# A step of a hybrid decoder with 64 experts: sample rows in slots of their own, gathered rows turned by VectorE, part of one expert's weights loaded earlier

## The reference

```python
scores = sigmoid(t @ w_router)                     # 64 experts
e_idx  = top 6 of (scores + b_router) in the best 4 of 8 groups
w      = scores[e_idx] / sum * 2.5
for each expert e: y += w[:, e] * (silu(t @ gate[e]) * (t @ up[e])) @ down[e]   # gate, up: 1024 x 256; down: 256 x 1024
y     += shared expert (same shape);  x = x + g2 * rms_norm(y)
```

## Time and profile before

| | |
|---|---|
| median of 3 runs | 930.7 us (930.54 to 934.95) |
| profiled execution | span 935.2 us |
| busy in it | PE 876.3, DVE 329.2, ACT 199.0, POOL 155.1 us |
| DMA | 325.47 MB, mean 348 GB/s |

### The profile page before, as it was taken

The page is one execution under the profiler, slowest core; times in us unless marked ns, Lnnn a source line. Parts: engine busy times, 40 slices in busy tenths (PEclk is TensorE's granted clock), DMA queues, the critical chain, the costliest instruction groups (busy, mean ns, idle before and its releaser), DMA issues.

```text
span 935.2 us, 18109 instructions
## 1 busy us (share of the span) xinstructions
PE 876.3 (94%) x7475; PEld 564.8 (60%) x7475; DVE 329.2 (35%) x795; ACT 199.0 (21%) x507; POOL 155.1 (17%) x185
## 2 busy tenths in 40 slices
PE   5899999997899899999899999999999999989987
PEld 3788888875666668756755555554555555444442
DVE  2315580047334598536322322222121221222214
ACT  2000110316222299024011111111111111101012
POOL 0000000022467000000312121121212212212110
PEclk9999999999899999999999999999999999999998
DMA  9966766737499947999999999999999999999993
GB/s 370 379 230 242 286 261 238 301 97 256 148 290 345 377 168 260 419 417 403 351 413 412 416 424 418 420 417 424 419 422 415 426 416 422 419 422 419 421 404 137
DMA packets 61237, 325.47 MB, mean 348 GB/s; under 512 B 16321, under 2 KB 25394, under 8 KB 40610
## 3 DMA queue, kind: packets, MB, share of 16 engines
q1 hardware_dynamic: 47218, 305.53, 81.4%
q0 software_dynamic: 12176, 18.56, 5.9%
q10 hardware_dynamic: 1760, 0.20, 0.2%
HBM read 326.65 MB, written 15.81 MB: 366 GB/s over the span
## 4 chain that ended last, share of the span: by engine, by line
PE 36%; DMA 13%; DVE 1%; SPq 0%; issue 0%; ACT 0%
PE bank L2428 19%; DMA slot_b<-in_w_e 13%; PE bank L2368 9%; PE bank L2379 4%; PE bank L2344 3%; PE bank L2438 1%; PE bank L2414 1%; SPq L1699 0%; DVE slot_b L2750 0%; DVE slot_b L2758 0%; PE bank L2398 0%; PE bank L2406 0%; ACT slot_b L2579 0%; DVE ht L2660 0%; DVE con L2652 0%
## 5 line engine op out<-in xcount | busy, mean ns | idle before, releaser
L420 PE MATMUL bank<-h,ring 128*128 128x264 f32 x608 | 138.4, 388 | 0.5 <-PE bank L420 0.3
L420 PEld LDWEIGHTS bank<-h,ring 128*128 128x128 f32 x608 | 114.6, 190 | 21.9 <-issue 2.6
L2652 DVE TENSOR_TENSOR con<-scales_of,bank 64x256 f32<-64x256 f32 x64 | 27.2, 425 | 270.5 <-ACT scales_of L2561 270.5
L1719 POOL DMA_INDIRECT xg<-tok_rows,tab_g x32 | 32.4, 1013 | 330.1 <-PE bank L2344 298.9
L2561 ACT ACTIVATE scales_of<-bank 64x256 f32<-64x256 f32 x64 | 24.2, 378 | 282.8 <-PE bank L2428 282.8
L2428 PE MATMUL bank<-done_out,xt 128*64 128x256 f32 x704 | 78.8, 381 | 3.7 <-DMA done_out<-in_w_e 2.8
L2428 PE MATMUL bank<-ring,xt 128*64 128x256 f32 x672 | 78.2, 386 | 0.0
L2428 PEld LDWEIGHTS bank<-done_out,xt 128*64 128x64 f32 x704 | 50.3, 137 | 33.9 <-issue 5.7
L2428 PEld LDWEIGHTS bank<-ring,xt 128*64 128x64 f32 x672 | 46.9, 138 | 35.7 <-issue 11.8
L2379 PE MATMUL bank<-sq,con 64*128 64x512 f32 x256 | 65.6, 609 | 0.0
L2368 PE MATMUL bank<-ring,ht 128*32 128x512 f32 x288 | 65.3, 595 | 0.0
(11 more groups left out here) (493 smaller groups left out, 1326.0 us busy)
## 6 DMA issues: line engine op xcount, KB each, us to landing
ring<-in_w_units SPq DMA_DIRECT2D x25, 2048.0 KB, 11.4
done_out<-in_w_e SPq DMA_DIRECT2D x22, 2048.0 KB
ring<-in_w_e SPq DMA_DIRECT2D x20, 2048.0 KB
slot_b<-in_w_e SPq DMA_DIRECT2D x11, 2048.0 KB
slot_f<-in_w_e SPq DMA_DIRECT2D x10, 2048.0 KB
ring<-in_w_e SPq DMA_DIRECT2D x16, 1024.0 KB
slot_b<-in_w_e SPq DMA_DIRECT2D x9, 1024.0 KB
done_out<-in_w_e SPq DMA_DIRECT2D x9, 1024.0 KB
```

Of the source, the lines that this page charges most:

```text
L420: mm = pe.matmul(bank[:, t % NB, 0:T], w[:, j, k, :], h[:, k, :], start=(k == 0), stop=(k == KD - 1))
L1719: pool.indirect_dma_start(xg[q % AHEAD][:, :], None, tok_rows, bass.IndirectOffsetOnAxis(ap=tab_g[:, q:q + 1].bitcast(U32), axis=0), bound ...
L2652: dve.tensor_tensor(hh[e % 2][:, :], sg[e % 2][:, :], bank[LB:2 * LB, 4 + e % 2, 0:FE], ALU.mult).then_inc(hh_ready, 1)
```

## The change

- The sample tokens no longer stand in the lists. Of every 32 places of an expert and half, 28 (`LS`) are for listed prompt tokens and 4 (`OWN`) hold always the same 4 sample rows, which are stored into xg once (8 small DMAs on POOL). VectorE adds their results to acc, with their weights of that expert, which may be zero (`add_own`). choice_rows, its scatters and its reading back are gone.
- The gathered rows are turned by VectorE in 32 x 32 blocks, straight from xg into one of two xt (`turn_rows`), PE's turn stays for the first pair only. ScalarE makes the copies `half_out` instead of VectorE.
- The two blocks of routing and expert loop are one, without the barrier between them.
- slot_f moves to a fixed place and holds only a gu. Of expert 5's, columns 1536 to 4096 of each partition (five eighths, 1.31 MB) are loaded in the state stage, the rest where the whole was. dn has 6 slots; expert 6's goes to w_sd.

```diff
-ROUNDS = -(-(P + TS) // HB)
+OWN = 4
+LS = HB - OWN
+ROUNDS = 1 + -(-(P - LS) // HB)
...
-SLOTS, DSLOTS = 6, 7
+SLOTS, DSLOTS = 6, 6
...
+AT_SLOT_F = AT_SAMP - 4 * GU
+EARLY_GU = 3 * 2 * FE
...
                         load_row(0)
                         load_row(1)
+                        sp.dma_start(slot_f[:, EARLY_GU:GU], io["w_e"][5][:, EARLY_GU:GU]
+                                     ).then_inc(small_in, 16)
                         sp.wait_ge(y_done6, 2)
...
-                        load_gu(sp, 5)
-                        load_dn(sp, 6)
+                        sp.dma_start(gu_at[5][:, 0:EARLY_GU], io["w_e"][5][:, 0:EARLY_GU]).then_inc(gu_in[5], 16)
...
+                        for i in range(AHEAD):
+                            for x4 in range(4):
+                                pool.dma_start(xg[i][x4 * HB + LS:(x4 + 1) * HB, :], rows_s[x4 % 2 * OWN:x4 % 2 * OWN + OWN, :]).then_inc(own_in, 16)
+                        pool.wait_ge(own_in, 16 * 4 * AHEAD)
...
+                        def turn_rows(q, h):
+                            if h == 0:
+                                dve.wait_ge(x_in[q % AHEAD], 16 * (q // AHEAD + 1))
                             if q >= 2:
+                                dve.wait_ge(gu_done, 2 * q - 3 + h)
                             for l in range(2):
+                                at = slice(h * LB + l * HB, h * LB + (l + 1) * HB)
+                                rows = xg[q % AHEAD][at, :].rearrange("p (k r c) -> p r k c", k=KD, r=4)
+                                for r in range(4):
+                                    ins = dve.transpose(xt[q % 2][32 * r:32 * r + 32, :, at], rows[:, r, :, :])
+                            ins.then_inc(xt_ready, 1)
...
+                        def add_own(q):
+                            dve.wait_ge(y_ready, 2 * q + 2)
+                            if q == 0:
+                                dve.wait_ge(own_ready, 1)
+                                ins = dve.tensor_scalar(acc[:, :], yo[q % NYO], own_w[:, q:q + 1], None, ALU.mult)
+                            else:
+                                dve.wait_ge(acc_ready, q)
+                                ins = dve.scalar_tensor_tensor(acc[:, :], yo[q % NYO], own_w[:, q:q + 1], acc[:, :], ALU.mult, ALU.add)
+                            ins.then_inc(acc_ready, 1)
```

More of the change, by code:

```diff
@@ L115 @@
                   ("valid", NT), ("later", NBLK - NE),
[L116 removed]
+                  ("count", MAXOVER), ("same_head", NH), ("code", NT), ("second", 1)):
     CONSTS[_name] = (_at, _at + _n)
@@ L1770, in _, with overflow @@
+                                        bounds_check=TP - 1, oob_is_err=False).then_inc(x_in[q % AHEAD], 16)
+            def overflow(eng):
+                eng.wait_ge(over_ready, 1)
+                return eng.value_load(over[0:1, 0:1], min_val=0, max_val=MAXOVER)
+            with nc.Block() as block:
                     @block.sync
@@ L1914, in _ @@
[L1914 to L1923 removed]
+                        pe.wait_ge(key_ready, 2)
@@ new lines, in combine @@
+                        def combine(n):
+                            q, h = n // 2, n % 2
+                            pe.wait_ge(y_ready, n + 1)
+                            pe.wait_ge(w_ready, q + 1)
+                            for l in range(2):
+                                at = slice(l * LB, (l + 1) * LB)
+                                mm = pe.matmul(bank[:, 2 * l + h, :], wmat[q % 2][at, :], yo[q % NYO][at, h * 512:(h + 1) * 512],
+                                               start=(q == 0), stop=(q == NPAIR - 1))
+                            mm.then_inc(comb_done, 1)
@@ new lines, in counts, with spread_weights @@
+                        def counts():
+                            for i, a in enumerate((0, 2)):
+                                mm = pe.matmul(bank[0:1, 7, (4 + i) * NE:(5 + i) * NE], ones[:, 0:1], chosen[:, a, :], start=True, stop=True)
+                            mm.then_inc(cnt_done, 1)
+                        def spread_weights():
+                            pe.wait_ge(comb_in, 32)
+                            pe.wait_ge(wgt_ready, 1)
+                            for i in range(2):
+                                mm = pe.matmul(bank[:, 7, 256:256 + NPAIR], own_at[i], wgt[0:TS, 1, i::2], start=(i == 0), stop=(i == 1))
+                            mm.then_inc(spread_done, 1)
@@ new lines, in _ @@
+                        act.wait_ge(fresh, 1)
+                        rows_half(0)
+                        rows_half(1)
+                        for e in range(NE):
+                            act.wait_ge(gu_done, e + 1)
+                            if e >= 2:
+                                act.wait_ge(hh_ready, e - 1)
+                            act.activation(sg[e % 2][:, :], bank[0:LB, 4 + e % 2, 0:FE], ACT.Silu).then_inc(sg_ready, 1)
+                            if e % 2 and e >= 2:
+                                half_out(e - 3)
+                                half_out(e - 2)
+                            if e == NE // 2:
+                                more = overflow(act)
@@ L1988, in _ @@
+                        act.wait_ge(sum_done, 1)
+                        square(4, slice(0, P), bank[:, 4, 0:QD], junk)
+                        act.wait_ge(sum_done, 2)
+                        act.activation(inv[:, 2:3], bank[:, 5, 0:1], ACT.Sqrt, bias=eps, scale=1.0 / D).then_inc(inv_rooted, 1)
+                        act.wait_ge(y_done, 3)
+                        for c in (2, 3):
+                            store(act, io["y"][TP:T, c * QD:(c + 1) * QD], y_s[32 * c:32 * c + TS, :])
                     @block.vector
```

1125 lines of the change are left out of this document (494 added, 631 removed).

## The result

The changed kernel takes **935.8 us** (median of 17 runs, 932.3 to 940.8), the kernel before 931.6 us (median of 17 beside it, 929.0 to 935.0). The ratio is **1.0044, 95% interval 1.0031 to 1.0058: 4.1 us slower**. The forecast was 927.8 us with 923.5 to 931.5 as its range, so it missed in direction as well as in range.

What follows compares the result with a forecast made beforehand. The queue of weights, at about 420 GB/s, was taken as the bound. The terms -3.1 - 1.2 + 1.9 + 0.3 - 1.4 + 0.65 = -2.9 us, from the 930.7 us median, gave 927.8 us, range 923.5 to 931.5.

Steps and rivals of the forecast that it cites:

- The bound: From 374 us the weight queue moves about 420 GB/s; remaining bytes, its idle time and the tail set the time.
- Step 1: Expert loop: PE no longer turns gathered rows, 1.36 us less a pair, counted for nothing except once in the tail.
- step 2: Expert loop: VectorE's turning takes 0.41 us each; costs nothing up to 0.67 us, a period of 14.4 us.
- cost 0: Expert loop: VectorE's 8.7 us latency fits PE's 7.06 + 3.57 us of work, 1.9 us left, so no cost.
- Step 3: State stage: 1.31 MB of expert 5's gate and up loaded early, fully hidden, -3.1 us.
- Step 4: Expert loop: scatters and gathering of the sample rows go away, 0.39 MB, -1.2 us (bounds 0.9 and 1.5).
- the own rows: Around 455 us: storing the sample rows once, 128 KB in 8 small stores of 16 KB, +0.3 us.
- Step 5: Around 455 us: less queued ahead, queue idles 5.5 us against 3.65, +1.9 us; later work joins without a gap.
- Hole 1: The weight queue's idle stretch before about 455 us, forecast between 444.8 and 455.3, 5.5 us idle against 3.65 before.
- the rival of small stores: Before the first gather: POOL's small stores hold it, gate_up(0) 3.5 us late, gain given back, 931.3 us; chance 0.14.
- Step 6: Tail: PE's path ends 3.1 us after the last weights, before 4.2, -1.4 us; later square-root table load, +0.65 us.
- The table load: Tail: ScalarE loads the square root's table behind the last copy, 1.28 us; squares start 1.1 us later, +0.65 us.

Runs made afterwards that it cites:

- experiment 11: Changed kernel plus 8 or 16 unused VectorE turnings of 32 x 192 in each pair from the fourth on: 937.3 us (one run) and 1080.7 us.
- experiment 1: Changed kernel with the first pair's gate products ahead of VectorE's turning of the second pair's rows: 1.0017 to the kernel before.
- experiment 8: Changed kernel plus 18 unused PE matmuls between the second gate and up and the turning of the products: 1.0015 to the kernel before.
- experiment 2: Changed kernel without the early load, expert 5's gate and up loaded whole in the routing stage: 1.0081 to the kernel before.
- experiment 12: First: changed kernel plus 18 unused PE matmuls in the first pair, 9 near the end, 1.0005. Second: the 9 on a changed kernel with further edits, 1.0009.
- experiment 5: Changed kernel with the square root's table load placed ahead of the last two half-expert outputs: 1.0044 to the kernel before.
- experiment 9: Changed kernel with the first pair's gate products ahead of the turning and the last half output copied by VectorE: 1.0018 to the kernel before.

## Why the prediction was wrong

- **The bound (queue of weights)**: right. From 480 us on the queue stands at 420 GB/s with all of VectorE's work beside it.
- **Step 1 and the loop of step 2**: right. PE caught up: it first waits for weights at 664 us, in place of 765. One turning takes 436 ns (0.41 taken), and experiment 11 bears out the slack (1.9 forecast, 2.0 measured) and the threshold of about 14.4 us, in so far as one run shows that 14.0 us cost nothing. The loop's period is 12.8 us and not the 12.45 of step 2: of the 1.36 us that step 1 takes away, 0.34 are turn_inner, which stays. It changes nothing, since the weights set the time. The other estimate of step 2, from twice 311 ns, is 0.62 us, only just under its bound of 0.67 and not well under it.
- **Step 2, "cost 0": the step that failed.** It took VectorE's in-order latency against "7.06 + 3.57 us of work" of PE, which is there in the loop and not in the first pair. There the two turnings hold the product, PE is idle for 4.29 us, its clock halves, expert 8's weights are issued late: hole 2, 2.5 us (experiment 1) or 2.7 us (experiment 8). The earlier trace rows have the steady loop only. The trace of before already shows such a fall in its first pair, behind the wait of 3.02 us in the earlier trace rows, where 32 matmuls take 4.77 us and the next 32 take 3.62:

```profile
460.34 4.77 PE L2428 MATMUL bank<-ring,xt 128*64 128x256 f32 x32
```

- **Step 3 (early part, -3.1)**: right in size, 3.4 us by experiment 2; the mechanism is different, since it works through the landing of GpSimd's gather as well.
- **Step 4 (-1.2) and the own rows (+0.3)**: with step 3 they should save 4.0 us of bytes; 4.7 us were saved.
- **Step 5, +1.9**: mis-sized. Hole 1 lost 6.9 us where 5.5 were forecast, on 3.65. Its timing was met: expert 6's weights were issued at 456.27 + 5.3 = 461.6 us, forecast 461.5. But "that joins the end of the queued work without a gap" held only until expert 8's issue. GpSimd's first gather was issued at 452.7 in the time of before, 2.7 us later than the 450 forecast, as the rival of small stores had it; that its rows landed in 3.7 us, the queue being half empty, made up for it.
- **Step 6, -1.4 + 0.65**: the gain did not come, and this is the second step that failed. PE's last combine starts at 922.12 + 5.3 = 927.5, 3.0 us later than the 924.48 of the earlier trace rows. PE's timeline from expert 61's gate and up on:

```profile
893.40 3.67 PE L2155 MATMUL bank<-slot_b,xt 128*64 128x256 f32 x32 [0.27 <-DMA slot_b<-in_w_e]
...
899.44 0.62 PE L2093 MATMUL bank<-ring,ht 128*32 128x512 f32 x2 [2.36 <-DMA x<-in_w_e]
...
922.12 1.99 PE L2104 MATMUL bank<-sq,con 64*128 64x512 f32 x8
```

  PE's way from there to the last combine is 28.7 us, near the 28.1 of step 6, and it was 924.48 - 897.76 = 26.7 before: the turn is gone (1.0 us), but a wait of 2.4 us for the downs of experts 58 and 59 and one of 0.4 us have come. That is +2.0 us, and the other profiles with the full clock there agree (experiment 12). To pay for it, expert 61's weights had to land 4.6 us earlier, 2.5 by the order of loads and 2.1 by the sum up to there. They landed at 503.4 us behind w_r, 502.4 before: 1.0 us later. In the five profiles that kept the clock in the first pair, had PE no later there than changed and left the loads alone (experiments 1, 5, 8, 9 and the first of 12) they landed at 500.0 to 500.2, so about 3.2 us of this is hole 2 as the profiled execution had it; why the rest of the 4.6 us is missing is open. The -1.4 also rested on a landing of the last weights at 920.3, worked out from 22.5 us of bytes and not read; the windows of before already move only 140 GB/s from 915 us on. The table load (+0.65) came as told:

```profile
922.26 0.58 ACT L2346 COPY sq<-bank 128x512 f32<-128x512 f32 x1 [1.13 <-PE bank L2093]
922.86 1.28 ACT L2373 ACT_TABLE_LOAD   x1
```

From the end of PE's last combine to the end it is 9.5 us, 8.7 before: 0.8 us.

By the repairs 2.5 to 2.7 us of the 4.1 are hole 2, each good to some 2 us. The profile splits its 3.7 us in another way: expert 61's weights 1.0 us later, PE's way from them to the last combine 2.0 us longer, the table load 0.8 us. Without hole 2 the first of these is 2.2 us earlier (experiment 1), and the end comes 0.6 us later than before. So the bytes saved and the new order of the last loads, less what hole 1 and the stretch ahead of it lose, bring expert 61's weights some 2 us earlier, and PE's longer way from there takes these back. Hole 2 and the table load are tested (experiments 1, 8 and 9, the latter by the profile alone); PE's longer way at the end is read from the profiles, and no run tests what would shorten it.

## What to carry to other kernels

Where an in-order engine takes over work, check its latency in the first turn of the loop, where the other engine has not yet the work that covers it elsewhere. An idle gap of TensorE can cost twice, once as a gap and again as half clock behind it (here 4.29 us, and 2.9 more); where the gap couldn't be closed, matmuls that filled it gave as much as closing it, as far as the intervals tell, and twice as many lost more than they gave. And where a transfer queue is the bound, price an edit by when each slot's next issue comes, not by bytes: bytes put into a hole here delayed the small gathers that release the issue after it. At the end of the kernel, read from the trace where the last weights land, and don't work it out from bytes.

## What was not expected of the hardware

- TensorE fell from 2.4 to 1.2 GHz behind an idle time of 4.29 us (10.08 us for 64 matmuls, granted clock 0.50, against 7.13), in experiment 11 behind the waits of 4.19 us, and never behind waits of 1.08 us or of 1.5 us. In the first pair it also fell behind waits of 1.78, 2.68, 3.10 and 3.42 us, and behind one of 2.4 us near the end in five of eleven profiles and not in six, from kernels that are the same there. So the length of the wait alone does not tell whether it falls. The Trainium skill (TensorE: Matmul & The Clock Gate, Part 1: The HAM clock gate) says that the array falls to 1.2 GHz when it has been idle and comes back once it is kept busy, which agrees with these rows, and that the number of slow matmuls at a kernel's start is "run-variable" for one and the same kernel; these rows show a like spread in the middle and at the end of one.
- From the issue of the same gather to PE's first use of its rows it took 3.7 us with the queue half empty and 7.9 us with it fuller (experiment 2); with small stores that landed 2.2 us later ahead of it, PE came to expert 0 7 us later. The median over the loop was 9.8 us before.
- The window 440 to 445 us shows a DMA share of 0.94 at 250 GB/s: here a busy share near 1 isn't a full queue, and only the GB/s tell that.
- VectorE's turning of 32 x 256 in fp32 takes 436 ns, where I took 410. And with VectorE busy for 277 of 414.6 us, most of it turning, GpSimd's gathers landed in 10.0 us in the median, against 9.8 before. By the Trainium skill (SBUF — State Buffer, the "DVE blocks DMA" trap) they would have lengthened if the turning ran in a 2-port mode; here they did not, by more than 0.2 us. Whether the turning runs in such a mode no run shows.
